# Loading x first, matrix products of ones while TensorE waits, and squares ahead of weight sums

## What is computed

```python
def rms_norm(x, g):
    y = xf * lax.rsqrt(jnp.mean(xf * xf, axis=-1, keepdims=True) + EPS)
    return y * g

# first_block, first operation
z = rmsnorm(h, mix_norm[j]) @ mix_w_in[j]

# second_block, per layer l
x = half_ffn(x, g_norm[l, 0], ...)          # half00, half10 (with the context rows)
h_lat = modulate(rms_norm(x, g_norm[l, 1]), ml[3], ml[4])   # mix0, mix1
x = half_ffn(x, g_norm[l, 2], ...)          # half01, half11

def half_ffn(h, g, shift, scale, gate, wg, wu, wd):
    return h + 0.5 * gate * swiglu(modulate(rms_norm(h, g), shift, scale), wg, wu, wd)
```

## Time and profile before

| what | value |
|---|---|
| runs | 3161.01, 3163.56, 3167.01 us |
| the profiled execution | 3160.99 us, its span 3159.5 us |
| granted TensorE clock, mean | 0.985 |
| PE busy | 2995.4 us (95%) |
| PE weight load busy | 2415.3 us (76%) |
| VectorE busy | 1375.0 us (44%) |
| ScalarE busy | 583.6 us (18%) |
| GpSimd busy | 37.3 us (1%) |
| DMA | 371.03 MB, mean 117 GB/s |

### The profile page before, as it was taken

The page is one execution under the profiler, slowest core; times in us unless marked ns, Lnnn a source line. Parts: engine busy times, 40 slices in busy tenths (PEclk is TensorE's granted clock), DMA queues, the critical chain, the costliest instruction groups (busy, mean ns, idle before and its releaser), DMA issues.

```text
span 3159.5 us, 43436 instructions
## 1 busy us (share of the span) xinstructions
PE 2995.4 (95%) x18294; PEld 2415.3 (76%) x18294; DVE 1375.0 (44%) x2855; ACT 583.6 (18%) x1342; POOL 37.3 (1%) x60
## 2 busy tenths in 40 slices
PE   7978899999899989999999899999999999999999
PEld 5756678898488968888844447888878888765899
DVE  3265433533533534445222625445244453225675
ACT  1232222113312021000021621010010000224110
POOL 0000000002000000000000000000000000000000
PEclk9989999999999999999999999999999999999999
DMA  6668754356244442222212112222422322331353
GB/s 223 214 215 284 273 172 159 109 185 174 80 137 140 128 159 75 86 64 74 90 56 75 54 40 67 80 74 63 117 80 80 93 61 74 108 103 44 123 156 106
DMA packets 355844, 371.03 MB, mean 117 GB/s; under 512 B 7395, under 2 KB 282228, under 8 KB 355524
## 3 DMA queue, kind: packets, MB, share of 16 engines
q1 hardware_dynamic: 350224, 358.24, 36.0%
q0 software_dynamic: 2208, 5.31, 0.9%
q10 hardware_dynamic: 3220, 4.71, 0.4%
HBM read 367.19 MB, written 1.05 MB: 117 GB/s over the span
## 4 chain that ended last, share of the span: by engine, by line
PE 89%; DVE 6%; ACT 3%; issue 2%; DMA 1%; ACTq 0%; DVEq 0%
PE acc L132 73%; PE aux L132 15%; ACT sb_xn L267 1%; PE aux L2150 1%; DVE sb_work L1415 0%; DMA weights<-mix_w_in 0%; DVE sb_work L1886 0%; DVE sb_work L1883 0%; ACT sb_work L1685 0%; ACT sb_work L1687 0%; DMA sb_x<-xT 0%; DVE sb_work L1897 0%; ACT sb_rstd L258 0%; DVE sb_work L1665 0%; ACT sb_rstd L260 0%
## 5 line engine op out<-in xcount | busy, mean ns | idle before, releaser
L132 PE MATMUL acc<-sb_xn,weights 128*128 128x256 f32 (+2 forms) x5184 | 1220.1, 391 | 31.4 <-ACT sb_xn L267 17.6
L132 PEld LDWEIGHTS acc<-sb_xn,weights 128*128 128x128 f32 x5184 | 951.2, 192 | 257.3 <-issue 136.0
L132 PE MATMUL acc<-sb_work 128*128 128x256 f32 (+1 forms) x1936 | 373.1, 346 | 0.0
L132 PEld LDWEIGHTS acc<-sb_work 128*128 128x128 f32 x1936 | 323.0, 191 | 34.1
L132 PE MATMUL acc<-sb_work,weights 128*128 128x256 f32 (+2 forms) x1508 | 322.4, 361 | 3.2 <-DVE sb_work L1200 1.4
L132 PE MATMUL acc<-sb_big,weights 128*128 128x256 f32 (+1 forms) x1776 | 313.8, 333 | 4.1 <-issue 3.9
L132 PEld LDWEIGHTS acc<-sb_big,weights 128*128 128x128 f32 x1776 | 278.1, 191 | 30.8 <-issue 5.3
L132 PEld LDWEIGHTS acc<-sb_work,weights 128*128 128x128 f32 x1508 | 254.2, 191 | 54.3 <-issue 26.1
L1415 DVE TENSOR_TENSOR sb_work<-weights 128x512 f32<-128x512 f32 (+1 forms) x112 | 99.7, 890 | 160.5 <-PE acc L132 160.4
L1387 ACT COPY sb_work<-acc 128x256 f32<-128x256 f32 (+1 forms) x112 | 37.9, 339 | 704.2 <-PE acc L132 704.2
L132 PE MATMUL aux<-sb_xn,sb_work 128*128 128x256 f32 (+1 forms) x704 | 153.2, 362 | 6.5 <-ACT sb_xn L267 6.5
(11 more groups left out here) (304 smaller groups left out, 2553.0 us busy)
## 6 DMA issues: line engine op xcount, KB each, us to landing
weights<-ffn_w_up SPq DMA_DIRECT2D x88, 1024.0 KB, 7.9
weights<-w_mod SPq DMA_DIRECT2D x36, 2048.0 KB, 9.0
weights<-ffn_w_down SPq DMA_DIRECT2D x48, 1408.0 KB, 7.1
weights<-ffn_w_gate SPq DMA_DIRECT2D x44, 1024.0 KB, 5.5
weights<-w_in SPq DMA_DIRECT2D x8, 2048.0 KB, 8.0
weights<-mix_w_in SPq DMA_DIRECT2D x6, 2048.0 KB, 13.5
weights<-na_w_qkv SPq DMA_DIRECT2D x6, 2048.0 KB, 9.9
weights<-ple_w_gate SPq DMA_DIRECT2D x4, 2048.0 KB, 8.2
```

The lines of the kernel that those rows point to most:

```text
L132: return te.matmul(o, lhsT, rhs, start=start, stop=stop, skip_group_check=True)
```

## The change

- ScalarE issues x before all else, then the four constants; the Hyena tables, `dft` and the context go to SyncE's queue, between the first weight blocks. GpSimd's two mask loads wait for x.
- TensorE no longer waits for the constants ahead of the first norm; it runs 22 products of ones by ones (128x128 by 128x128, into `aux3`, never read) first, and 8 more between the norm and the first group.
- ScalarE's Silu of the condition, and VectorE's three small constant-dependent operations, stand behind the first norm instead of ahead of it.
- In the four half FFNs and the two mixings, 11 such products of ones stand between the norm's products and the next.
- `vector_norm` is split; in `vector_half_ffn` the squares stand ahead of the weight sums.

```diff
-    def vector_norm(N):
-        W = T2 - N.t0
+    def vector_squares(N):
         if N.extra:
             ve.wait_ge(N.extra[0].sem, N.extra[1])
         for k in range(1, KT, 2) if not N.hooked else ():
...
+    def vector_norm(N, constants=False):
+        vector_squares(N)
+        if constants:
+            ve.wait_ge(const_in.sem, 64)
+        vector_scaled(N)
+
+    def vector_scaled(N):
         ve.wait_ge(rstd_set.sem, N.rstd)
+        W = T2 - N.t0
...
+    def tensor_idle(n):
+
+        for _ in range(n):
+            mm(aux[3][:, 0:128], ones[:], ones[:])
+
     def tensor_mix_in():
         tensor_norm(mix_norm)
+        tensor_idle(8)
+        te.wait_ge(const_in.sem, 64)
...
     def gpsimd_masks():
         msk_at = ins["c_masks"]
+        gp.wait_ge(x_in.sem, 16)
...
     def tensor_half_ffn(F, following=None):
         tensor_norm(F.norm)
+        tensor_idle(11)
...
     def vector_half_ffn(F):
+        vector_squares(F.norm)
         sig, value = F.norm.x_ready[KT - 1]
         ve.wait_ge(sig.sem, value)
         vector_weight_sums(F.fast, 0, (0, 1, 2, 3))
...
         vector_scales(F.l, 0 if F.j == 0 else 2, F.m0 + 8)
-        vector_norm(F.norm)
+        vector_scaled(F.norm)
...
     def tensor_mixing(M):
         tensor_norm(M.norm)
+        tensor_idle(11)
...
     def sync_program():
         sp.wait_ge(x_in.sem, 16)
-        sync_wide(mix_in, ins["mix_w_in"][0])
+        sync_wide(mix_in[0:1], ins["mix_w_in"][0])
+        for dst, src in (<the six Hyena tables>):
+            hy_in.on(sp.dma_start(dst, src))
+        sync_wide(mix_in[1:3], ins["mix_w_in"][0])
+        ctx_in.on(sp.dma_start(dft, ins["c_dft"]))
+        sync_wide(mix_in[3:4], ins["mix_w_in"][0])
+        ctx_in.on(sp.dma_start(x[:, :, 0:CTX], ...))
+        sync_wide(mix_in[4:], ins["mix_w_in"][0])
...
     def tensor_program():
-        te.wait_ge(const_in.sem, 64)
         te.wait_ge(ones_set.sem, 1)
+        tensor_idle(22)
...
     def scalar_program():
-        for sig, loads in (<constants, Hyena tables, x, dft, context>):
+        x_in.on(ac.dma_start(x[:, :, CTX:T2], ...))
+        for dst, src in (<the four constants>):
+            const_in.on(ac.dma_start(dst, src))
+        scalar_norm(mix_norm)
         ac.wait_ge(const_in.sem, 64)
         sil_set.on(ac.activation(sil[:, :, 0:2], ..., ACT.Silu))
-        ac.preload_act_table_set(NAT_LOG)
-        scalar_norm(mix_norm)
...
     def vector_program():
         v_step.on(ve.memset(eps_col, EPS))
         eps_set.on(ve.memset(gn_eps, GN_EPS))
-        ve.wait_ge(const_in.sem, 64)
+        vector_norm(mix_norm, constants=True)
         v_step.on(ve.memset(sil[:, :, 2:32], 0.0))
...
-        vector_norm(mix_norm)
```

More of the change, by code:

```diff
@@ L2317, in sync_program @@
         sp.wait_ge(x_in.sem, 16)
-        sync_wide(mix_in, ins["mix_w_in"][0])
+        sync_wide(mix_in[0:1], ins["mix_w_in"][0])
+        for dst, src in ((feats[0:17], ins["c_feats"]), (fw[0:17, 0, :], ins["hy_f_w1"][0]), (fw[0:64, 1, :], ins["hy_f_w2"][0]),
+                         (fw[0:64, 2, :], ins["hy_f_w3"][0]), (w4[0:64], ins["hy_f_w4"][0]), (decay, ins["c_decay"])):
+            hy_in.on(sp.dma_start(dst, src))
+        sync_wide(mix_in[1:3], ins["mix_w_in"][0])
+        ctx_in.on(sp.dma_start(dft, ins["c_dft"]))
+        sync_wide(mix_in[3:4], ins["mix_w_in"][0])
+        ctx_in.on(sp.dma_start(x[:, :, 0:CTX], ins["ctxT"].rearrange("(k p) t -> p k t", p=128)))
+        sync_wide(mix_in[4:], ins["mix_w_in"][0])
         sync_modulation()
@@ L2372, in scalar_program @@
     def scalar_program():
[L2373 to L2381, removed]
+        x_in.on(ac.dma_start(x[:, :, CTX:T2], ins["xT"].rearrange("(k p) t -> p k t", p=128)))
+        for dst, src in ((col[:], ins["cols"]), (ident[:], ins["c_ident"]), (blk64[:], ins["c_blk64"]), (headm[:], ins["c_headm"])):
+            const_in.on(ac.dma_start(dst, src))
+        scalar_norm(mix_norm)
         ac.wait_ge(const_in.sem, 64)
         sil_set.on(ac.activation(sil[:, :, 0:2], cols("cond", 16).rearrange("p (k s) -> p k s", s=2), ACT.Silu))
-        ac.preload_act_table_set(NAT_LOG)
-        scalar_norm(mix_norm)
         scalar_mix_in()
```

## The result

| | before | after |
|---|---|---|
| runs beside each other, median (lowest to highest), us | 3165.28 (3161.01 to 3170.11) | 3143.22 (3138.01 to 3145.03) |
| profiled execution, its span, us | 3160.99, 3159.5 | 3138.01, 3136.7 |
| granted TensorE clock, mean | 0.985 | 0.991 |
| PE busy, us | 2995.4 | 3006.3 |

The account below looks back on a forecast made before the run. TensorE, 89% of the chain, was taken as the bound, so only its waits and low-clock time could be won: start 12.3, squares 5.0, 4.7 and 5.65, ones 1.7 and 1.7, in all 31.1 us, giving 3132 us, range 3125 to 3142.

Parts of the forecast that it names:

- The squares' place: Norms of half00, half01 and half11: squares ahead of the weight sums gain 5.0, 4.7 and 5.65 us.
- Ones ahead of `mix0` and `half11`: Ones in the norm's wait hold the clock high for what follows: 1.7 us gained at each.
- No low stretch is left: Rival: clock stays high after the first product in half00, half01 and half10 too; 5.2 us more, 3127; 9 in 100.
- The start, sizes: Start: x landing at 5.9 us, first weights at 14.1, group 1 ending at 17.6; 12.3 us gained.
- loads behind cost little: Start: loads queued behind x hardly delay it, as 7.0 us was reckoned and 6.8 measured with 2 MB behind.
- group 1 at clock 1.00: Sign of being right, at the start: group 1 runs at the high clock, 3.5 us in place of 6.05.
- What follows is a chain of its own and moves with it: After group 1: three filter steps on VectorE come earlier with the start, so its 12.3 us gain carries through.
- Slower: Rival: earlier work brings clock falls at other recurrence waits, 1.6 us each; from 23 falls on slower, 3170; 2 in 100.
- nothing ties the waits to the start: Recurrence: argument against the slower case, that its short TensorE waits don't depend on the start.
- one fall in 240 us was all: Recurrence, 190 to 430 us: the clock fell only once before, 0.84 over ten us, 1.6 us lost.
- The sum again: Whole kernel: the forecast sum was 12.3 + 5.0 + 4.7 + 5.65 + 1.7 + 1.7 = 31.1 us gained.

Follow-up runs that it names:

- e4: The changed kernel with all products of ones left out, at the start and in the second block; 3134.68 us, ratio 0.9904.
- e2: The kernel before with only the squares put ahead of the weight sums, no ones, old start; 3146.00 us, ratio 0.9948.
- e1: The changed kernel's new start, with its 22 and 8 ones, but the second block as in the kernel before; 3161.67 us, ratio 0.9990.
- e10: The changed kernel without ones at the start, plus 7 ones (3 in half11) between each half FFN's first and second product; 3128.33 us, 0.9893.
- e11: The changed kernel with 47 small products (94 records) at the start in place of the 22 and 8 ones; 3134.40 us, ratio 0.9908.
- e6: The changed kernel without the 22 and 8 ones at the start, keeping the 11 at each place in the second block; 3130.52 us, ratio 0.9892.
- e8: The changed kernel with 15 small products (30 records) at the start in place of the 22 and 8 ones; 3141.97 us, ratio 0.9929.

## Why the prediction was off

- **The squares' place:** right in mechanism and size. 5.0, 3.9 and 5.85 us against 5.0, 4.7 and 5.65; e4, without the low stretch of the changed kernel's `half01` section, has 4.8 there. e2 gives the same without the rest.
- **Ones ahead of `mix0` and `half11`:** right. 1.7 and 2.0 against 1.7 and 1.7; e4, without ones, has neither (125.53 and 216.4). `mix1` was taken at nothing and brought 0.5. The 1.9 us in the section ahead of it lie in the FFN of `half10`, where the clock did not fall behind the first product (the rival "No low stretch is left", at one place of three); e4, without ones, has them as well (414.53), so they are not shown to be the ones' doing.
- **The start, sizes:** 10.2 against 12.3. x landed at 6.8, 6.05 us from its issue where 5.2 were forecast and 4.7 for x alone. The constants behind it in the queue are the likely reason ("loads behind cost little" was wrong then), but no run leaves them out. The weights landed 9.2 us after their issue where 8.2 were taken, at 16.0. The wait for the weights then hid what the ones brought, 2.0 us of the norm. In single executions (e1, e10, e11) filter step 0 was later, at 21.4 to 22.2, because group 1 took 5.38 us at the low clock in place of 3.69. In e1 that happened with all the ones at the start in place, behind a wait of 2.0 us for the weights, so the ones did not secure "group 1 at clock 1.00".
- **The step that failed** is "What follows is a chain of its own and moves with it". The start was costed by where its products lie in time, and the 30 of ones at nothing. They also count as instructions: they moved the ends of TensorE's instruction blocks from the modulation's products into the recurrence's chain. The recurrence grew by 6.6 us, 4.9 of them TensorE's longer busy time at the lower clock behind these stalls and 1.7 idle time. The rival "Slower" named the recurrence and the clock as the place; it had the low stretches, but not the stalls ahead of them, nor that the count of products at the start decides where those fall. Its "nothing ties the waits to the start" was false, and so was "one fall in 240 us was all": the window from 192 to 206 of the kernel before shows 0.52. That the kernel before had 8.1 us of waits without a cause there was in its trace, and I had not asked what ended them.
- **The sum again:** with 10.2 for 12.3, -6.6 for the recurrence, and the rest as forecast, 31.1 becomes 22.4; 22.1 were measured between the medians and 23.0 between the profiled executions. That it fits so closely is partly luck: the other sections, at which nothing was forecast, moved by -0.9 to +1.9 us and nearly cancel.

The version to keep is e6: the change without the ones at the start, 3130.52 us, 0.9892 (0.9878 to 0.9905).

## What to carry to other kernels

Instructions put into a wait can be free in time and still shift everything that is fetched behind them: look in the waits of the busiest engine for "issue" entries at even distances in its instruction count, and see on which side of a serial chain they fall before and after the edit, and whether the clock falls behind them. Not every "issue" wait is one of these: all executions here have four more, two of 2.0 us and two of 0.4, from 590 to 1130 us, which stand at the same products whatever is put ahead of them. An edit that only fills a wait is worth its place only if what follows the wait is not bound by something else; here the weights were, and the version without the filler gained 12.7 us over the changed kernel. When a gain at one place does not arrive at the end, cut both executions into sections and look for the one that got longer.

## What the runs showed of the chip

- TensorE stalled 0.2 to 2.6 us at ends of instruction blocks of 126 or 127 records (253 instructions with the weight loads, 16.4 KB), while the DMA engines were 0.66 to 0.69 busy: 8.1 us in seven stalls in the kernel before, 8.9 in six in the changed one, 13.5 in e8, 2.5 with the DMA share at 0.23. The Trainium skill, "Runtime: NRT & Kernel Launch", section on instruction fetch mechanics, says that instructions come in blocks of 16 KiB, 256 each; the 253 counted here agree nearly. It also says that crossing a block is mostly hidden. In most of this kernel, where a block lasts 14 us or more, that holds; in the recurrence, with 6 to 7 us for a block, it doesn't.
- The granted clock fell behind 18 of 32 stalls of 1.0 us or more in the recurrence's chain. TensorE was busy 8.00 us of 8.00 in the windows that show 0.57 (242 and 406), so a low clock says nothing about idle time inside the stretch. It was at 0.66 from 37 to 42, with 5.00 of 5.00 busy, behind three waits of 1.3 to 1.4 us for ScalarE that ended at 25.3, 30.9 and 36.4.
- Raising the clock ahead of the first norm shortened the norm from 5.65 (e4) to 3.62 us, and filter step 0 came no sooner (19.57 in e4, 19.64 in the changed kernel).
